# GpSimd in place of VectorE for the normalization of one layer's attention probabilities, with the entry of the second block and the first modulation steps reordered

## The reference, cut to what matters

```python
# first block, layers 0 and 1 (layer 1 is "layer 2" of the title)
ml = ada_mod(c, w_ada[l], b_ada[l], 6)            # silu(c) @ w_ada + b_ada; c_ctx likewise
zl = modulate(x, ml[0], ml[1]) @ w_in[l] + b_in[l]
...
s = einsum('bqhgd,bkhd->bhgqk', qi, k_all) * ATTN_SCALE    # 8 heads, 4 blocks of 128 queries, 768 keys
p = softmax(s, axis=-1)
o = einsum('bhgqk,bkhd->bqhgd', p, v_all)
...
# second block, layers 2 and 3
u = rmsnorm(h, ln_mix[i]) @ w_in[i]
```

## Time and profile before

| | |
|---|---|
| median of 3 runs | 3149.74 us (3148.41 to 3151.05) |
| profiled execution | 3147.84 us, of which the span is 3146.0 us |
| granted TensorE clock, mean | 0.995 of full |
| PE busy | 3065.3 us, 97% |
| DVE busy | 1980.2 us, 63% |
| ACT busy | 1153.0 us, 37% |
| POOL busy | 808.0 us, 26% |
| chain that ended last | PE 88%, DVE 6%, ACT 2% |

### The profile page before, as it was taken

One profiled execution on the slowest core, in us unless ns is written; L12 is line 12 of the kernel. 1 busy time (PEld: TensorE's weight loads), 2 busy tenths in 40 slices (PEclk: granted clock), 3 DMA queues, 4 the chain that ended last, 5 costly groups with the idle time before them and its releaser, 6 DMA issues.

```text
span 3146.0 us, 43692 instructions
## 1 busy us (share of the span) xinstructions
PE 3065.3 (97%) x16056; PEld 2599.2 (83%) x16056; DVE 1980.2 (63%) x2784; ACT 1153.0 (37%) x1661; POOL 808.0 (26%) x330
## 2 busy tenths in 40 slices
PE   7999999999999999999999999999999999999998
PEld 5999887899999999997777677778887686777766
DVE  5899987644676154356989985763646566445443
ACT  3113364234243221224334535443223635443443
POOL 0001212223323232231012024512445332233312
PEclk8999999999999999999999999999999999999999
DMA  7442001112212212123541022423233212122211
GB/s 280 175 173 87 28 1 61 47 61 101 78 63 65 75 60 67 61 67 134 195 163 54 1 67 87 144 81 100 94 100 108 71 61 76 54 80 74 81 57 67
DMA packets 77709, 275.25 MB, mean 87 GB/s; under 512 B 8688, under 2 KB 11888, under 8 KB 76656
## 3 DMA queue, kind: packets, MB, share of 16 engines
q1 hardware_dynamic: 70800, 253.94, 23.9%
q10 hardware_dynamic: 6752, 19.14, 1.7%
HBM read 266.75 MB, written 6.29 MB: 87 GB/s over the span
## 4 chain that ended last, share of the span: by engine, by line
PE 88%; DVE 6%; ACT 2%; issue 1%; DVEq 1%; DMA 1%; SPq 0%; ACTq 0%
PE ps L684 53%; PE ps L1065 11%; PE ps L619 4%; PE ps L633 2%; PE ps L800 2%; PE ps L1207 1%; PE ps L872 1%; PE ps L963 1%; PE ps L788 1%; PE ps L993 1%; PE ps L1286 1%; DVE small L2355 1%; PE ps L691 1%; PE ps L1304 1%; PE ps L1016 1%
## 5 line engine op out<-in xcount | busy, mean ns | idle before, releaser
L550 POOL TENSOR_TENSOR w_lo<-w_raw,w_hi 128x1024 fp32r<-128x1024 f32 x308 | 791.1, 2572 | 2197.5 <-ACT w_hi L1394 2197.5
L1394 ACT ACTIVATE w_hi<-w_raw 128x1024 fp32r<-128x1024 f32 x376 | 395.8, 1056 | 564.4 <-PE ps L684 286.2
L684 PE MATMUL ps<-act_hi,w_hi 128*128 128x384 f32 (+1 forms) x2544 | 529.0, 356 | 4.3 <-DVE w_lo L2181 2.5
L684 PE MATMUL ps<-act_lo,w_hi 128*128 128x384 f32 (+1 forms) x2544 | 519.1, 352 | 0.0
L684 PE MATMUL ps<-act_hi,w_lo 128*128 128x384 f32 (+1 forms) x2544 | 518.5, 352 | 0.0
L684 PEld LDWEIGHTS ps<-act_hi,w_hi 128*128 128x128 f32 x2544 | 450.8, 188 | 70.0 <-issue 34.4
L684 PEld LDWEIGHTS ps<-act_lo,w_hi 128*128 128x128 f32 x2544 | 454.3, 188 | 32.2 <-issue 0.5
L684 PEld LDWEIGHTS ps<-act_hi,w_lo 128*128 128x128 f32 x2544 | 454.3, 188 | 32.0
L2249 DVE SCALAR_TENSOR_TENSOR x<-ps,mod,x 128x384 f32<-128x384 f32 (+1 forms) x128 | 64.2, 546 | 277.4 <-PE ps L684 222.7
L2412 DVE SCALAR_TENSOR_TENSOR x<-arena,vec,x 128x512 f32<-128x512 f32 x336 | 228.2, 707 | 0.0
L2404 DVE SCALAR_TENSOR_TENSOR arena<-arena,vec 128x783 f32<-128x783 f32 (+1 forms) x240 | 226.2, 943 | 0.0
(11 more groups left out here) (380 smaller groups left out, 4556.7 us busy)
## 6 DMA issues: line engine op xcount, KB each, us to landing
w_raw<-in_weights SPq DMA_DIRECT2D x376, 512.0 KB, 3.5
arena<-in_ada_w SPq DMA_DIRECT2D x75, 512.0 KB, 4.8
tmp<-in_ada_w SPq DMA_DIRECT2D x21, 512.0 KB, 6.1
x<-in_x SPq DMA_DIRECT2D x2, 1536.0 KB, 19.2
x<-in_x ACTq DMA_DIRECT2D x1, 3072.0 KB, 10.3
arena<-in_pool_w ACTq DMA_DIRECT2D x2, 1024.0 KB, 4.9
x_mid<-x ACTq DMA_DIRECT2D x1, 2048.0 KB, 7.1
x<-x_mid ACTq DMA_DIRECT2D x1, 2048.0 KB, 8.7
```

The lines of the kernel that those rows point to most:

```text
L550: nc.gpsimd.tensor_tensor(WL[:, w], raw, WH[:, w].bitcast(f32), ALU.subtract).then_inc(units_split, 1)
L684: last = nc.tensor.matmul(tile(o, o + b - a), w[:, s * UNIT + k * P:s * UNIT + (k + 1) * P], act[:, k * TOK + a:k * TOK + b], start=(n == ...
L1394: nc.scalar.activation(WH[:, s * UNIT:(s + 1) * UNIT], RAW[:, (s % 2) * UNIT:(s % 2 + 1) * UNIT], ACT.Copy).then_inc(hi_done, 1)
```

## The change

1. **Multiplication.** In layer 1 of the first block DVE only inverts the sum and signals it (`attn_r`); POOL waits for that signal and multiplies the 128 x 768 buffer. For this, POOL's split of round `RING[1, "u"]` stands ahead of the 32 multiplications. Layer 0 stays as it was.
2. **Modulation steps.** The table's entry at unit 2 of layer 0 is at unit 3 now.
3. **Entry of the second block.** `ina` uses PSUM tiles 0, 2, 1, 0 for its four units in place of 0, 1, 2, 1. For layer 3 the second part of the column sums is made at chunk 3 of `ina` and no longer at the end of `pg`, and ACT copies it behind the last chunk's preparation.

```diff
-    STAGES += [((_l, "ina"), 4, (1, 2, 1, 0)), ...
+    STAGES += [((_l, "ina"), 4, (2, 1, 1, 0)), ...
-ADA_AT = ({u: (u - 2, u - 1) for u in range(2, 3 * CH + 1, 2)},
+ADA_AT = ({max(u, 3): (u - 2, u - 1) for u in range(2, 3 * CH + 1, 2)},
@@ in2
-                return "ina", n, (0, 1, 2, 1)[n], n // 3
+                return "ina", n, (0, 2, 1, 0)[n], n // 3
@@ gpsimd
+            def normalized(l, it):
+                pool.wait_ge(on(l, "attn_r"), it + 1)
+                p = TMP[:, it % 2 * TOK:(it % 2 + 1) * TOK]
+                nc.gpsimd.tensor_scalar(p, p, SMALL[:, 6 + it % 2:7 + it % 2], None, ALU.mult).then_inc(on(l, "attn_p"), 1)
...
-            low_halves(RING[1, "qkv"] + 1, RING[1, "u"])
-            if 1 in HALVED:
-                attention_lows(1)
-            low_halves(RING[1, "u"], RING[1, "up0"] + 1)
+            low_halves(RING[1, "qkv"] + 1, RING[1, "u"] + 1)
+            for it in range(4 * HEADS):
+                normalized(1, it)
+            low_halves(RING[1, "u"] + 1, RING[1, "up0"] + 1)
@@ paired (PE, second block)
+                    tiles = (0, 2 if st == "ina" else 1)
                     for s in range(2):
                         pe.wait_ge(units_split, nth_done(l, st, s))
-                        pe.wait_ge(tile_free[s], taken(l, st, s, 0))
+                        pe.wait_ge(tile_free[tiles[s]], taken(l, st, tiles[s], 0))
...
-                            last = products(ps(s, 0, SEQ), w, act, ...
+                            last = products(ps(tiles[s], 0, SEQ), w, act, ...
@@ sums_between (PE)
+                    if l > LAYERS and k == 3:
+                        part_sums(l, "rms1", range(4, 7))
@@ end of pg (PE)
                             ple_in_context(gbank(3), 0).then_inc(ple_mm, 1)
-                        part_sums(l + 1, "rms1", range(4, 7))
+                        else:
+                            part_sums(l + 1, "rms1", range(4, 7))
@@ end of pg (ACT)
-                part_copied(l + 1, "rms1")
+                if l > LAYERS:
+                    part_copied(l + 1, "rms1")
                 nc.scalar.preload_act_table_set("natural_log_exp_and_others")
                 act.wait_ge(*at_least(l, "h_out", CH))
                 next_input(l + 1, CH - 1)
+                if l == LAYERS:
+                    part_copied(l + 1, "rms1")
@@ normalized (DVE, first block)
-                    V.reciprocal(SMALL[:, 6 + it % 2:7 + it % 2], SMALL[:, 2 + it % 2:3 + it % 2])
+                    r = V.reciprocal(SMALL[:, 6 + it % 2:7 + it % 2], SMALL[:, 2 + it % 2:3 + it % 2])
+                    if l:
+                        return r.then_inc(on(l, "attn_r"), 1)
```

More of the change, by code:

```diff
@@ L98 @@
 for _l in range(LAYERS, 2 * LAYERS):
-    STAGES += [((_l, "ina"), 4, (1, 2, 1, 0)), ((_l, "gv"), 4, (0, 0, 1, 1)), ((_l, "inb"), 15, (9, 8, 0, 0)), ((_l, "gla_o"), 0, (0, 0, 1, 1)),
+    STAGES += [((_l, "ina"), 4, (2, 1, 1, 0)), ((_l, "gv"), 4, (0, 0, 1, 1)), ((_l, "inb"), 15, (9, 8, 0, 0)), ((_l, "gla_o"), 0, (0, 0, 1, 1)),
                ((_l, "uq"), 5, (9, 8, 0, 0)), ((_l, "mla"), 0, (4, 4, 4, 4)), ((_l, "w_out"), 8, (4, 4, 0, 0))]
@@ L1078, in paired @@
                                 pe.wait_ge(*at_least(l, ready[i // 2], ready[2](k)))
-                            last = products(ps(s, 0, SEQ), w, act, slot_of(l, st, s) * UNIT + k * P, n, k, i == 0 and at_ == 0, i == 2 and at_ == CH - 1)
+                            last = products(ps(tiles[s], 0, SEQ), w, act, slot_of(l, st, s) * UNIT + k * P, n, k, i == 0 and at_ == 0, i == 2 and at_ == CH - 1)
                             if i == 2 and at_ == CH - 1:
```

## The result

The changed kernel takes **3173.22 us** (the median of four executions: 3171.8, 3171.97, 3174.48 and one disturbed one of 6960.35, which the ratio leaves out). The kernel before took 3149.53 us beside it (3148.41 to 3151.05). The ratio is 1.0076, 95% interval 1.0063 to 1.009. The prediction was 3153.8 us with a range of 3145 to 3162; the kernel is slower by 23.7 us, outside the range and on the side that had a chance of 0.28.

What follows compares the result with a forecast made beforehand. In layer 1's attention the path over DVE (6.89 us for two tiles) and PE (6.88) were taken as level. +7.3 (multiplication) - 2.3 (steps) - 0.9 (entry) = +4.1 us on 3149.7 gave 3153.8 us, range 3145 to 3162.

Steps and rivals of the forecast that it cites:

- the chain over DVE: Layer 1 attention: transposes, scores, maximum, bias and two taps, inverse, multiplication, back to transposes; 6.89 us for two tiles, no slack.
- PE's own work: Layer 1 attention: 3.44 us a tile when nothing is late, 6.88 us for two tiles.
- the formula: Layer 1 attention with the multiplication on POOL: two tiles take 6.37 + X us, nothing lost up to X = 0.51, 14 pairs.
- X: Time of POOL's multiplication of one tile in layer 1's attention: estimated 1.04 us, between 0.62 and 1.86; +7.3 us in all.
- the ring: Layer 1 attention's two-tile cycle from transposes through maximum, inverse and multiplication to the next transposes: 6.89 us, forecast 7.41 with POOL.
- The first multiplication: Start of layer 1's attention: waits for POOL's split until 1704.4, ends 0.7 us later than DVE's; a chunk boundary covers it.
- Change 2: Layer 0, steps 0 and 1 moved to unit 3: unit 2 starts without a wait, -2.3 us; ends 0 and -2.4.
- the cover of 0.8 us: Layer 0: the later-issued load lands at 71.2 us, 0.8 before unit 4 needs it; failing costs at worst 2.3 us.
- Change 3: Entry of layer 3: PE's wait for the square of chunk 6 goes, column sums only move; -0.9 us, ends 0 and -1.9.
- The dear multiplication: Rival, between inverse and transposes of the 32 tiles: POOL's multiplication costs 1.86 us, kernel 3165.3 us; chance 0.28.
- DVE's queue is the pace: Rival, layer 1 attention: DVE's queue sets the pace, all 6.8 us of waits go, kernel 3139.7 us; chance 0.08.
- The cheaper X: POOL's multiplication at the skill page's one-input line rate: 0.86 us a tile, +4.9 us instead of +7.3.

Runs made afterwards that it cites:

- DVE's halves: Multiplication back on DVE, in two 384-column instructions, first three transposes waiting only for the first, against the changed kernel: 3144.94 us, ratio 0.9988 to the kernel before.

## Why the prediction was wrong

- **What bounds: nearly right.** The prediction put the chain over DVE at 6.89 and PE's own work at 6.88, and called them level. The first is borne out by undisturbed pairs of 6.90. The second isn't: with DVE's halves, which took 0.2 us out of the first chain, a pair took 6.76. The 3.44 us that were read as a tile with nothing late still held 0.06 of waiting. It changes nothing in the sum, which goes by the chain over DVE.
- **The place of the loss and the formula: right.** At five values of X from 1.19 to 2.21 an undisturbed pair takes 6.27 to 6.30 + X, where the formula has 6.37: inverse and step to POOL took 0.25 us and not 0.34. 14 pairs by (2.205 - 0.51) are 23.7 us; 24.3 were measured between the maxima. That they are so near is partly luck: the ring made 22.6 of it, and the fall of the clock at 1716 us the other 1.7, for which the prediction had no term. What makes the clock fall there isn't shown: it also fell at 1712 us with the multiplication on DVE in halves, and it didn't with 384 or 256 columns on POOL.
- **X: the step that failed.** The prediction took 1.04 us, by halving the slope of the subtraction because one operand less is read, and 1.86 as the upper end. Measured: 2.205. The halving had no row behind it, and the two-operand form, cheaper at 1.466, has shown that fewer operands don't lower the price. The end was wrong too, as it interpolated between 256 and 1024 elements, though the kernel before has POOL at this very shape, two instructions of 2.247 and 2.301 us (one line's view, kernel before):

```profile
L561 POOL TENSOR_TENSOR w_lo<-arena,w_hi x2: 2247/2274/2301, 359.3 to 361.5; 128x768 fp32r<-128x768 f32 x2
```

  With that row as X, the formula gives 14 x (2.274 - 0.51) = 24.7 us. The measured X in place of 1.04 makes 14 x (2.205 - 1.04) = 16.3 us, of the 19.4 by which the forecast missed. Why the one-operand form is the dearer one stays open.
- **The end of the stage: a term left out**, 2.7 us. Behind the last maximum there are two multiplications with nothing left to hide them, one of them 3.2 us long beside taps; the transposes wait 3.57 us at 1836.87.
- **The first multiplication: right**; it started at 1704.32, against 1704.4. With the longer X the fourth maximum came 0.6 us later than before, counted from the first, and the fifth was back, so the chunk boundary covered it as forecast.
- **Change 2: right where it is made, wrong at the end.** -2.1 from the last matmuls ahead of unit 2, against -2.3, and no wait at unit 4 in the kernel after; but in seven of the ten traces with the change the steps at unit 4 took up to 0.9 us longer, so the cover of 0.8 us isn't safe. Then a fall of the clock took 1.7 of it. The prediction had no term for such falls, though the kernel before has one (0.57 in 3032 to 3036).
- **Change 3: right**, -0.92 against -0.9. The start of `ina` was forecast 1.9 us earlier; it is 2.0 (2818.18, with the 26.6 that the kernel came in behind).
- **The rivals.** The dear multiplication was the right one, but its price of 3165.3 us stopped at 1.86. Its worse form, contention with taps, played hardly a part (1.0 us of the 2.7 behind the last maximum), though from X = 1.59 on the two do meet: the one-operand instruction let 18 of 19 taps through. "DVE's queue is the pace" was kept too far apart from the forecast: DVE is idle between the tiles, but the taps in its queue are 1.32 of the 8.50 us, and they weigh only because the wait for POOL makes the ring the bound.
- **The skill's rule.** The cheaper X that the page promised (the Trainium skill, GPSIMD Engine Reference, Engine selection: one input at roughly line rate) isn't borne out: 2.2 us for 768 elements a partition, 3.6 times VectorE's 0.62. For two inputs the page's rule of about twice as slow is near: against 0.96 us of VectorE's own two-operand instruction of 128 x 768, GpSimd's subtraction of 2.27 is 2.4 times as slow and its multiplication with a repeated column, 1.47, 1.5 times.

## What to carry to other kernels

Price an operation on an engine that hasn't done it by the row of that engine with the same shape, at full cost, and halve nothing for fewer operands; and if no such row exists, ask what the sum is at the dearest row rather than at a line between others. Look at a multiplication that is moved off a busy engine as a link of a chain: what counts is when its result is there, and what the freed engine does ahead of the next link (here two taps) becomes part of the price once another engine waits. GpSimd isn't free because it is idle: it had nothing to do in this stage, and the move still cost 27 us.

## What was not expected of the hardware

- GpSimd's multiplication of 128 x 768 fp32 by a column: 2.205 us; by a constant 2.129; as a two-operand instruction with a repeated column 1.466. At this shape the form of the instruction matters more than what it reads.
- A two-operand tap of VectorE that starts while GpSimd's one-operand multiplication runs is hardly ever held (18 of 19 at 0.74 to 0.75 us); beside the two-operand one, twice, it was (1.95 us). By the Trainium skill (SBUF — State Buffer, Who interferes with whom), a VectorE instruction with two SBUF inputs contends with a GpSimd instruction that reads SBUF; the second case agrees, and so does the multiplication of 3.21 us that started within a tap; the 18 taps don't.
- GpSimd's 384 columns took 1.447 us when VectorE multiplied 384 beside it and 1.243 when it didn't: 0.20 us lost. Its 256 columns took 1.194 beside VectorE's 512, where 0.92 is the estimate from 0.28 us and 2.5 ns an element: 0.27 lost. VectorE's own multiplications took 0.42, 0.486 and 0.62 us for 384, 512 and 768 columns, 0.52 ns a column, which makes 0.20 and 0.27 us as well. So GpSimd lost just the part of VectorE's time that grows with its columns, and VectorE's 384 lost nothing (0.42 us with GpSimd beside them or without).
- The granted clock fell to 0.50 behind a gap of 2.46 us in PE's work near 1482 us in eleven of thirteen traces (the kernels before and after and the eleven here), and did not behind the same gap in the other two. In the kernel after it was 0.50 from 1716 to 1718 us too, within the attention, behind a window in which PE was busy for 1.00 of 2.00 us. A fall cost 1.7 us at either place, about as much as change 2 gains and more than change 3 does.
